# First attention of a two-block transformer kernel: values behind the scores, reciprocals turned at a step's end

## What is computed

```python
def dilated_branch(q, k, v, window, dil):
    ...
    s = jnp.where(valid[None, :, None], s, -jnp.inf)
    m = jnp.max(s, axis=-1, keepdims=True)
    e = jnp.exp(s - m)
    den = jnp.sum(e, axis=-1, keepdims=True)
    p = e / den
    o = jnp.einsum("bnhqk,bnkhd->bnqhd", p.astype(vw.dtype), vw)
    ...
def dilated_mixture(q, k, v):
    for window, dil in ((128, 1), (512, 4), (2048, 16)):
        ...
    w = jax.nn.softmax(jnp.stack(lses, axis=0), axis=0)
    o = jnp.sum(w[..., None] * jnp.stack(outs, axis=0).astype(jnp.float32), axis=0)
```

## Time and profile before

| what | value |
|---|---|
| median of 3 runs | 3314.73 us (3313.18 to 3315.9) |
| profiled execution, span from first to last instruction | 3315.1 us |
| instructions | 52199 |
| PE busy | 3218.8 us, 97% |
| DVE busy | 1648.7 us, 50% |
| ACT busy | 1122.1 us, 34% |
| POOL busy | 994.1 us, 30% |
| mean granted TensorE clock | 0.986 of full |

### The profile page before, as it was taken

One profiled execution on the slowest core, in us unless ns is written; L12 is line 12 of the kernel. 1 busy time (PEld: TensorE's weight loads), 2 busy tenths in 40 slices (PEclk: granted clock), 3 DMA queues, 4 the chain that ended last, 5 costly groups with the idle time before them and its releaser, 6 DMA issues.

```text
span 3315.1 us, 52199 instructions
## 1 busy us (share of the span) xinstructions
PE 3218.8 (97%) x20554; PEld 2851.7 (86%) x20554; DVE 1648.7 (50%) x2786; ACT 1122.1 (34%) x2097; POOL 994.1 (30%) x688
## 2 busy tenths in 40 slices
PE   8999999999999999999999999999999999799997
PEld 6677768788888888899899899999999999799997
DVE  5554556755554545666666623255555043522223
ACT  3433333333322214555555531155455110300002
POOL 3112224787772323222222142200100222122221
PEclk9999999999999999999999999999999999899998
DMA  4011112122234112000000012100000221478888
GB/s 158 26 32 33 33 64 102 64 77 77 77 103 190 45 44 97 20 24 23 20 20 20 14 46 84 67 25 28 24 22 20 90 85 56 179 248 310 312 310 293
DMA packets 80581, 294.97 MB, mean 89 GB/s; under 512 B 11298, under 2 KB 16226, under 8 KB 77200
## 3 DMA queue, kind: packets, MB, share of 16 engines
q1 hardware_dynamic: 67296, 243.92, 20.8%
q0 software_dynamic: 6160, 18.63, 2.3%
q10 hardware_dynamic: 6944, 29.90, 2.3%
HBM read 239.39 MB, written 47.70 MB: 87 GB/s over the span
## 4 chain that ended last, share of the span: by engine, by line
PE 56%; DVE 2%; ACT 1%; issue 1%; DMA 0%; POOL 0%; SPq 0%; POOLq 0%; ACTq 0%; DVEq 0%
PE PS L658 14%; PE PS L3104 7%; PE PS L3566 7%; PE PS L646 6%; PE PS L3168 4%; PE PS L3596 4%; PE PS L3320 4%; PE PS L3135 3%; PE PS L3397 3%; PE PS L3362 3%; PE PS L3169 0%; PE PS L3117 0%; PE PS L3333 0%; PE PS L3398 0%; DVE affT L2957 0%
## 5 line engine op out<-in xcount | busy, mean ns | idle before, releaser
L680 POOL CAST w_hi<-ring 128x1024 fp32r<-128x1024 f32 x130 | 135.8, 1044 | 1572.9 <-PE PS L658 407.2
L682 POOL TENSOR_TENSOR w_lo<-ring,w_hi 128x1024 fp32r<-128x1024 f32 x130 | 332.4, 2557 | 10.5
L2215 ACT ACTIVATE EA<-EA,small_sb 128x1040 f32<-128x1040 f32 x144 | 166.6, 1157 | 186.1 <-DVE small_sb L2634 186.0
L2634 DVE CUSTOM_DVE_ANT_0 EA<-PS,biasH,low_a 128x1024 f32<-128x1024 f32 x128 | 163.7, 1279 | 57.8 <-PE PS L3135 57.7
L3104 PE MATMUL PS<-u_hi,w_hi 128*128 128x348 f32 x504 | 173.5, 344 | 0.0
L3104 PE MATMUL PS<-u_lo,w_hi 128*128 128x348 f32 x504 | 162.1, 322 | 0.0
L3104 PE MATMUL PS<-u_hi,w_lo 128*128 128x348 f32 x504 | 161.9, 321 | 0.0
L1611 DVE TENSOR_TENSOR hid_lo<-hid,hid_hi 128x1024 fp32r<-128x1024 f32 x44 | 92.1, 2133 | 118.5 <-ACT hid_hi L1253 118.5
L1703 PE MATMUL PS<-u_hi,w_hi 128*128 128x512 f32 x352 | 147.0, 418 | 3.0 <-POOL w_lo L682 2.3
L1900 PE MATMUL PS<-t_hi,slot_hi 128*128 128x512 f32 x352 | 138.8, 394 | 5.6 <-DVE t_lo L1512 3.9
L3168 PE MATMUL PS<-Va,PTa 128*128 128x128 f32 (+1 forms) x1152 | 139.9, 275 | 0.0
(11 more groups left out here) (496 smaller groups left out, 8314.6 us busy)
## 6 DMA issues: line engine op xcount, KB each, us to landing
ring<-in_stream SPq DMA_DIRECT2D x130, 512.0 KB, 3.7
w_gate_sb<-in_w_gate SPq DMA_DIRECT2D x64, 512.0 KB, 7.1
w_up_sb<-in_w_up SPq DMA_DIRECT2D x64, 512.0 KB, 8.1
w_down_sb<-in_w_down SPq DMA_DIRECT2D x64, 512.0 KB
gu_raw<-in_gate_up SPq DMA_DIRECT2D x22, 1024.0 KB, 5.7
hid_keep<-hid_out SPq DMA_DIRECT2D x17, 512.0 KB, 2.9
hid<-hid_keep ACTq DMA_DIRECT2D x15, 512.0 KB, 16.6
x_keep<-xT ACTq DMA_DIRECT2D x1, 4176.0 KB, 14.6
```

What stands on the lines that cost most here:

```text
L680: pool.tensor_copy(w_hi[j][:, :, :], w_raw[j][:, :, :]).then_inc(S["w_rounded"], 1)
L682: pool.tensor_tensor(w_lo[j][:, :, :], w_raw[j][:, :, :], w_hi[j][:, :, :], ALU.subtract).then_inc(S["w_split"], 1)
L2215: act.activation(e[0:m, :], e[0:m, :], ACT.Exp, scale=-1.0, bias=small[0:m, 8 + 2 * par + k:9 + 2 * par + k], accum_out=small[0:m, 12 + 2 ...
L2634: dve.tensor_tensor_reduce(e[0:m, 0:T1], wide(2 * k, T1, m), bias, -1.0, low_a[0:m, t, k:k + 1], ALU.add, ALU.min, low).then_inc(S["aa_max ...
```

## The change

Five moves within the loops, no other edit. On PE, `values(g - 1)` goes from a step's end to right behind `scores(g + 2)` at every step, and `turn_recips` goes from the step after, behind `turn_probs(g + 1, 0)`, to the end of its own step, behind `turn_probs(g, 1)`. On DVE, `result(g - 1)` (with the addition of squares in it) goes from behind `recip_rows(g)` to the step's start. On ACT, `spread_recips` goes from behind taps, squares and the turned V to the step's start. No instruction is added or removed, and no wait is changed.

```diff
@@ ScalarE, step g
                     woven = woven_unit(pp, s)
+                    if g and chunks[(g - 1) % NS][1] == 0:
+                        spread_recips(NT * ((g - 1) // NS) + chunks[(g - 1) % NS][0])
                     if pp + 1 < DCT:
...
                         square_result(NT * ((g - 2) // NS) + chunks[(g - 2) % NS][0])
-                    if g and chunks[(g - 1) % NS][1] == 0:
-                        spread_recips(NT * ((g - 1) // NS) + chunks[(g - 1) % NS][0])
@@ VectorE, step g
                     pp, s = divmod(g, NS)
+                    if g and (g - 1) % NS in last_chunk.values():
+                        result(g - 1)
                     take_probs(g)
                     if g + 2 < DCT * NS:
                         scores(g + 2)
                     if chunks[s][1] == 0:
                         recip_rows(g)
-                    if g and (g - 1) % NS in last_chunk.values():
-                        result(g - 1)
@@ TensorE, step g
                     if g + 2 < DCT * NS:
                         scores(g + 2)
+                    if g:
+                        values(g - 1)
                     if s == 0 and g:
-                        values(g - 1)
                         turn_values(pp)
                     turn_probs(g, 0)
-                    if g and chunks[(g - 1) % NS][1] == 0:
-                        turn_recips(g - 1)
                     if woven and late:
                         unit(*woven, 0)
                     if woven:
                         unit(*woven, 1)
                     turn_probs(g, 1)
-                    if s:
-                        values(g - 1)
+                    if chunks[s][1] == 0:
+                        turn_recips(g)
```

## The result

The changed kernel took **3353.32 us** (median of 4 runs, 3348.89 to 3356.38), the kernel before on the same chip 3315.14. The ratio is 1.0115, with a 95% interval from 1.0103 to 1.0128: slower, by 38.2 us where 29.6 were forecast.

A forecast was written before the change was run, and what follows sets the result against it. PE, busy 97% of the span, was taken as the bound. Added waits, matmul order and clock, 15.6 + 9.6 + 2.2 + 0.8 + 0.9 - 2.5 + 3.0 = 29.6, onto 3314.7 gave 3344.3 us; range 3331 to 3357.

The forecast's parts named there:

- term 1: Steps 0 to 2, all four passes: PE waits about 1.3 each for DVE's row of reciprocals, +15.6 us.
- term 2: Step 4: values behind the scores wait for ACT's spread reciprocals, 2.7 in passes 0 to 2, 1.5 in pass 3, +9.6.
- 3, first scores of a pass: Step 0 at three pass boundaries: PE's scores wait 0.74 for DVE's evictions, +2.2 us.
- Term 4: Steps without units: longer waits for DVE's chain, +0.8 in pass 0 and +0.9 at the end of pass 3.
- Term 6: Granted clock falls after two of the four step 4 waits, at 1.4 us lost each: +3.0 (0 to 6).
- Term 5: Order of PE's matmuls: transposes more often followed by units or another transpose, at most 0.1 in 48 steps, -2.5.
- the rival of 3361: The clock falls after the short waits too, 12 times 1.4 more: 3361 us, 10%.
- the third rival: DVE's addition of squares, now ahead of the copy, collides; 2.1 falls on PE three to six times, 3351 to 3357, 8%.
- DVE's waits before `result`: Sign: DVE's waits before `result`, 43.5 us in all before, fall far below that, with no gain.
- The first rival: Early `result` frees DVE; PE's waits of 4.81 and 1.19 and two low-clock stretches go: 3306 us, 4%.
- ACT in time: Square roots could move up as DVE is free sooner; the step 4 waits and their clock go: 3331.7 us, 8%.

The follow-up runs named there:

- e1: The changed kernel with the row of reciprocals turned one step later, behind that step's first half unit: 3334.43 us, ratio 1.0053.
- e9: The changed kernel with DVE writing the row of reciprocals ahead of the scores of step g+2 instead of behind them: 3330.76 us, ratio 1.0047.
- e2: The changed kernel with ACT spreading tile 3's reciprocals in step 3, ahead of the square roots and table load, not in step 4: 3339.71 us, ratio 1.0070.
- e4: The changed kernel with ACT's move undone, `spread_recips` again behind taps and squares: 3352.75 us, ratio 1.0110.
- e5: The changed kernel with the edits of e1 and e2 together: 3324.05 us, ratio 1.0027.
- e3: The changed kernel with DVE's move undone, `result(g - 1)` again behind `recip_rows`: 3352.53 us, ratio 1.0111.
- e8: The changed kernel with both edits of e5 and DVE's order of before: 3323.40 us, ratio 1.0023.
- e10: The changed kernel, all five moves kept, with the edits of e9 and e2 and e7's shift of reciprocals: 3315.00 us, ratio 1.0000.
- e7: The kernel before, with DVE's 512-column reciprocals for k's second half and q one step later in pass 0: 3309.50 us, ratio 0.9981.

## Why the prediction was right or wrong

The direction, the mechanism of the main terms and the range held. The terms, in the profiled execution (+39.5):

| | forecast | measured |
|---|---|---|
| 1, row too early, steps 0 to 2 | 15.6 | 4 x (1.15 + 1.28 + 1.28) = 14.8 |
| 2, values behind step 4's scores | 9.6 | 3 x 2.66 + 1.30 = 9.3 |
| 3, first scores of a pass | 2.2 | 3 x 0.68 = 2.0 |
| 4, pass 0, step 6 | 0.8 | 5.10 + 0.23 - 4.81 = 0.5 |
| 4, end of pass 3 (all waits from step 6 on) | 0.9 | 10.1 - 6.5 = 3.6 |
| unforeseen: step 2 of pass 3 | 0 | 1.15 |
| 6, clock | 3.0 | 15.7 - 5.0 = 10.7 |
| 5, order of matmuls | -2.5 | the rest, -2.6 |

**Terms 1, 2 and 3** came within 0.2 us of each wait, in the places named; e1, e9 and e2 show their causes by taking them away. Reading PE's end of transposes against DVE's and ACT's next free moment in the trace of before was enough. Step 0 was "a little less" by 0.13, as said. That the values of step 4 wait for the end of one chain on ACT, not for the transposes, is shown by e2: the spread ahead of the table load ended the wait.

**Term 6 was mis-sized**, and is most of the miss: 10.7 us for 3.0. What it priced came as forecast: low clock followed two of the four waits of term 2, and lost clock behind them is 3.2. The short waits of term 1 left the clock at 1.00 throughout, so that the rival of 3361 (10%) is out. The step that failed is that the falls were priced for term 2 alone. The end of pass 3, where PE's waits grew as well, got nothing: from 440 us on in the trace of before and from 470 here, lost clock is 3.4 and 10.5, which is 7.1 of the 10.7. Nor is the price of a fall, taken from the earlier trace rows as 1.4, a constant. Behind the wait of 3.05, low clock lasted from about 473.5 to 487 and took 6.2. Behind the same wait of 3.04 to 3.06 it took 4.9 in e1, but 1.4 to 1.7 in e2, e4 and e5. Over the ten experiments lost clock was between 2.9 and 14.2. The changed kernel's own times spread over 7.5 us, and this profile was the longest of them, so that against its median the miss is about 1.3 less.

**Term 4's end of pass 3 was mis-sized** by 2.7. The larger part is one collision: the addition of squares at 470.31 took 1.93 for 0.28, inside POOL's subtraction of 469.73 to 472.09, right ahead of the copy, evictions and row on which PE stood for 3.05. In e3, where the addition stands behind the row, the wait is 1.79. That is the third rival, with its place and its mechanism; ahead of a copy it happened once, not three to six times, and the argument that the moved additions come too late for POOL's split holds for the other places.

**The wait of 1.15 at step 2 of pass 3 was not foreseen.** It is term 2's mechanism at another place: values stand early and wait for the end of a chain on ACT. That chain hangs on DVE's addition for the convolution (431.57), which took 2.88 inside POOL's subtraction where it took 0.68 before. But the collision as such is not new. Before, it fell on the addition of squares just ahead:

```profile
407.75 2.29 DVE L1427 TENSOR_TENSOR attn_acc<-attn_acc,y_sq 128x128 f32<-128x128 f32 x1
409.96 0.68 DVE L1378 TENSOR_TENSOR conv_acc<-conv_acc,rs 128x512 f32<-128x512 f32 x1
```

So ACT was let go just as late behind DVE's row, 3.3 us before and 3.1 now; what changed is that PE asks for the values sooner. In e3 and e8 it is again the squares that collide, and the wait stays (1.04 and 2.85); in e9 nothing collides there, and it is gone. The same addition took 2.90 and 2.89 in passes 1 and 2 (209.61, 321.38) without a wait of PE. The Trainium skill (SBUF — State Buffer, Who interferes with whom) has the rule, and the trace agrees: the long instructions read two operands in SBUF, and the multiplication of 470.11, with one operand in SBUF and one in PSUM, kept its 0.29 inside the same subtraction.

**Term 5** stands in the table as what is left over. It can be read directly where the clock stayed at 1.00: from the first scores of pass 2 to those of pass 3 the changed kernel takes 110.19 us (301.97 to 412.16) for 103.84, and its added waits in between are 7.05, so that the order gives back 0.7 a pass. That bears out the -2.5.

**DVE's waits before `result`** were forecast to fall far below 43.5 and rose to 72.3. I took it that an earlier place in PE's queue brings the values nearer to DVE; but DVE's own place moved up by more, and PE's waits came ahead of them. That nothing is gained there was right, and e3 and e8 show it: with DVE's order undone the time is the same within the noise.

The first rival (early `result` frees DVE, 3306) is out with e3, e8 and e10. That the wait of 4.81 in the earlier trace rows came from reciprocals of 512 columns is shown by e7; the other one, 1.19 in pass 3, stays in e7, and no run bears on its cause. "ACT in time" is out: the roots did not move up. What stays open is why low clock follows a given wait in one run and not in another. No run here was made for it alone.

## What to carry to other kernels

Before an instruction is moved towards its producer, list what the producing queue has ahead of the release at that moment; a wait on a reused buffer in that list ties the release to the consumer's own last work, and then the consumer waits at every step. A long wait of an engine that is half idle is no target: look for what the bound engine waits for, and move that (here two halves of a normalisation, one step later). A wait of the bound engine can carry a second price in clock, which in these traces came to anything from nothing to twice the wait itself; forecast it as a range of that width, and for every wait that grows, not only for the largest term. The length of the wait alone did not decide it. The twelve waits of 1.15 to 1.28 at steps 0 to 2 cost no clock, those of 2.66 cost it in two cases of three, and in e10 a wait of 0.94 at 139.77 was followed by 1.7 us of lost clock.

## What the runs showed of the hardware that was not expected

The granted clock stayed at 0.50 (1.2 of 2.4 GHz) for twelve us in which PE was busy 11.55, with transposes, scores, values and 16 matmuls of one column; after 5.10 us of waiting it was back at about 156, some 4 us after PE resumed. Filling the wait with 13 matmuls held it at 1.00, so the fall could be prevented, and that stretch became 5.6 us shorter; but a wait of 2.66 that had kept its clock before was followed by low clock in that run. A DVE addition of 128 x 128, 0.28 us at the median, took 1.93 beside POOL's subtraction of 2.36 (470.31), as a delay that fell on PE through the instructions queued behind it. Where DVE's addition began first, by 0.26 us (e9, 416.12), it took 0.73 where 0.68 is usual, and POOL's subtraction took 2.72 for 2.40.
